# Conditioning panels of a two-block transformer kernel: partial products moved from TensorE to VectorE

## The reference

```python
s_c, s_cc = silu(c), silu(c_ctx)
for i in range(2):
    m  = (s_c  @ ada_w[i] + ada_b[i]).reshape(1, 9, 1, D)     # ada_w: 2 x 1024 x 9216
    mc = (s_cc @ ada_w[i] + ada_b[i]).reshape(9, D)
    x = half_step_ffn(x, m[:, 0], m[:, 1], m[:, 2], ...)      # ctx too, with mc[0..2], in layer 0
    hx = modulate(x, m[:, 3], m[:, 4])                        # hc: ctx with mc[3], mc[4], in layer 0
    y = neighbourhood_attention(hx, hc, ...) if i == 0 else short_conv_mixer(hx, ...)
    x = post_norm_update(x, y, m[:, 5], ...)
    x = half_step_ffn(x, m[:, 6], m[:, 7], m[:, 8], ...)
```

## Time and profile before

| | |
|---|---|
| three runs | 3009.21, 3017.51, 3021.42 us; median 3017.51 |
| profiled execution | 3014.72 us, of which the span of the trace is 3012.9 |
| busy, share of the span | TensorE 96%, weight load 84%, VectorE 59%, ScalarE 45%, GpSimd 12% |
| transfers | 474.79 MB, mean 158 GB/s |
| mean granted TensorE clock | 0.99 |

### The profile page before, as it was taken

The page is one execution under the profiler, slowest core; times in us unless marked ns, Lnnn a source line. Parts: engine busy times, 40 slices in busy tenths (PEclk is TensorE's granted clock), DMA queues, the critical chain, the costliest instruction groups (busy, mean ns, idle before and its releaser), DMA issues. The chain is left out here.

```text
span 3012.9 us, 51229 instructions
## 1 busy us (share of the span) xinstructions
PE 2898.0 (96%) x19396; PEld 2540.7 (84%) x19396; DVE 1765.8 (59%) x2644; ACT 1356.7 (45%) x1928; POOL 375.3 (12%) x306
## 2 busy tenths in 40 slices
PE   6999999899999999999899999999999999999998
PEld 3667765677888889888899989899999998988998
DVE  2323224267766667666545866757855577566784
ACT  1222213125655544554344544455644454436563
POOL 2111100113110110211100120201101002020110
PEclk8999999999999999999999999999999999999999
DMA  9986354751565655465435505245555451533564
GB/s 325 285 252 195 103 164 130 198 168 49 158 184 154 194 183 160 148 195 182 142 120 167 161 28 176 92 134 153 170 162 161 137 154 57 160 114 112 161 179 135
DMA packets 586157, 474.79 MB, mean 158 GB/s; under 512 B 28721, under 2 KB 547889, under 8 KB 585665
## 3 DMA queue, kind: packets, MB, share of 16 engines
q1 hardware_dynamic: 584464, 460.44, 49.8%
q0 software_dynamic: 1520, 11.95, 1.3%
HBM read 471.23 MB, written 4.72 MB: 158 GB/s over the span
## 5 line engine op out<-in xcount | busy, mean ns | idle before, releaser
L2309 DVE TENSOR_TENSOR low<-raw,high 128x1024 fp32r<-128x1024 f32 (+1 forms) x744 | 904.6, 1219 | 801.0 <-ACT high L2079 798.6
L2079 ACT CAST high<-raw 128x1024 fp32r<-128x1024 f32 (+1 forms) x744 | 768.1, 1034 | 987.9 <-PE PS L1987 604.7
L1985 PE MATMUL PS<-NHh,high 128*128 128x272 f32 (+1 forms) x2304 | 669.0, 290 | 11.4 <-DVE NHl L1752 6.9
L1987 PE MATMUL PS<-NHh,low 128*128 128x272 f32 (+1 forms) x2304 | 660.8, 287 | 0.0
L1986 PE MATMUL PS<-NHl,high 128*128 128x272 f32 (+1 forms) x2304 | 660.0, 286 | 0.0
L1985 PEld LDWEIGHTS PS<-NHh,high 128*128 128x128 f32 x2304 | 433.3, 188 | 16.9 <-issue 9.1
L1986 PEld LDWEIGHTS PS<-NHl,high 128*128 128x128 f32 x2304 | 433.9, 188 | 0.8
L1987 PEld LDWEIGHTS PS<-NHh,low 128*128 128x128 f32 x2304 | 433.6, 188 | 0.0
L1983 PE MATMUL PS<-XX,high 128*128 128x512 f32 x966 | 347.8, 399 | 0.0
L1985 PE MATMUL PS<-XX,high 128*128 128x512 f32 (+1 forms) x752 | 273.5, 364 | 6.9 <-DVE XX L2370 4.4
L1982 PE MATMUL PS<-XX,low 128*128 128x256 f32 x966 | 272.4, 282 | 1.4 <-DVE XX L2370 1.0
(11 more groups left out here) (351 smaller groups left out, 4868.7 us busy)
## 6 DMA issues: line engine op xcount, KB each, us to landing
raw<-w_in_dram SPq DMA_DIRECT2D x416, 256.0 KB, 3.0
raw<-ffn_w_in_dram SPq DMA_DIRECT2D x352, 256.0 KB, 3.4
part<-ada_w_dram SPq DMA_DIRECT2D x184, 256.0 KB, 4.2
raw<-w_ffn_in_dram SPq DMA_DIRECT2D x176, 256.0 KB, 3.2
raw<-ffn_w_out_dram SPq DMA_DIRECT2D x160, 256.0 KB, 3.1
raw<-w_branch_dram SPq DMA_DIRECT2D x96, 256.0 KB, 3.0
raw<-w_ffn_out_dram SPq DMA_DIRECT2D x80, 256.0 KB, 3.0
part_sg<-ada_w_dram SPq DMA_DIRECT2D x48, 256.0 KB, 3.0
```

What stands on the lines that cost most here:

```text
L1985: nc.tensor.matmul(out, wh, xh, start=begin, stop=False)
L1987: last = nc.tensor.matmul(out, wl, xh, start=False, stop=end)
L2079: nc.scalar.copy(high[:, slot, 0:nk, :], raw[:, slot, 0:nk, :]).then_inc(s_high, 1)
L2309: nc.vector.tensor_tensor(low[:, slot, 0:nk, :], raw[:, slot, 0:nk, :], high[:, slot, 0:nk, :].bitcast(F32), ALU.subtract).then_inc(s_low, 1)
```

## The change

All panels but the first four are no longer multiplied on TensorE. VectorE multiplies each 128x512 row tile of a part by the matching column of silu(c) (a value for each partition) and adds it to an accumulator of 128x512 in SBUF, one for each panel of the turn; panels 4 to 9 (`ADA_BOTH`) have a second accumulator with silu(c_ctx). This is done in `split_low`, behind the low copy of chunk `HOST[A]` + 4. Once for each turn TensorE sums the accumulators over the partitions against a mask with a single column of ones (`ada_sum`), two chunks behind the host of the turn's last part, at the latest behind chunk 83. SyncE's wait for a part buffer is now for VectorE's accumulation (`s_adak`). The parts are spread anew: 16 over chunks 2 to 13, 16 over 14 to 23, 16 over 24 to 33, 8 over 34 to 39, 72 over 45 to 82. They use 14 buffers: four (later two) during glu, seven from chunk 45, three from 68. The rule of `issue` for a buffer that was used before is the same.

```diff
-ADA_HOSTS = ((0, 32, 80), (44, 24, 24), (68, 16, 24))
+ADA_HOSTS = ((2, 12, 16), (14, 10, 16), (24, 10, 16), (34, 6, 8), (45, 38, 72))
+ADA_BOTH = 10
...
-    return HOST[4 * TURN * t - 1]
+    return min(HOST[4 * TURN * t - 1] + 2, 83)
...
+        ROWS, TAIL, TOP = range(4, 11), 11, (12, 13)
+        part_slot = [A % 4 if HOST[A] < 32 else A % 2 if HOST[A] < 44 else
+                     ROWS[A % 7] if HOST[A] < 68 else 11 + A % 3 for A in range(ADA_PARTS)]
+
+        def ada_acc(t, x, c):
+
+            if c:
+                return acc_both[:, x, :]
+            return (acc2, acc3)[x - 2][:] if x > 1 else (RS if t < 5 else SG)[:, x, :]
...
-            due = HOST[before] + 4 if before is not None else {PSG: 47, PRS: 47, TAIL: 71}.get(part_slot[A], 1)
+            due = HOST[before] + 4 if before is not None else 3 + part_slot[A] if HOST[A] < 44 else 48 if HOST[A] < 68 else 71
...
                 if before is not None:
-                    sp.wait_ge(s_ada, 4 * ADA_FIRST + before + 1)
-                elif slot == PSG:
-                    sp.wait_ge(s_hl, FT + 2)
+                    sp.wait_ge(s_adak, before + 1)
+                elif slot in ROWS:
+                    sp.wait_ge(s_chunk, steps[1]["S0"] + 4)
                 elif slot == TAIL:
                     sp.wait_ge(s_chunk, steps[2]["S0"] + 4)
-                elif slot < 3:
+                elif slot in TOP:
+                    sp.wait_ge(s_res, KT + 4)
+                elif slot == 0:
                     sp.wait_ge(s_ada, 4 * ADA_FIRST)
...
+            def ada_sum(t):
+
+                pe.wait_ge(s_adak, 4 * TURN * t)
+                pe.wait_ge(s_adarow, max(1, t - 1))
+                for c in range(2):
+                    for x in range(TURN):
+                        both = TURN * t + x < ADA_BOTH
+                        if both or not c:
+                            last = nc.tensor.matmul(PS[32 * x:32 * x + 32, ROW_BANK + t % 2, :],
+                                                    ONEW[:, 2 * (TURN - x) - 1 - c:2 * (TURN - x) + 31 - c], ada_acc(t, x, c),
+                                                    start=not c, stop=bool(c) or not both)
+                last.then_inc(s_adasum, 1)
...
-                        for A in ada_parts(S + c):
-                            ada_part(ADA_FIRST + A // 4, A % 4)
+                        if isinstance(S, int) and S + c in sum_after:
+                            ada_sum(sum_after[S + c])
...
                 nc.vector.tensor_tensor(low[:, slot, 0:nk, :], raw[:, slot, 0:nk, :],
                                         high[:, slot, 0:nk, :].bitcast(F32), ALU.subtract).then_inc(s_low, 1)
+                for A in ada_parts(S - NSLOT if isinstance(S, int) else S):
+                    ada_accumulate(A)
+
+            def ada_accumulate(A):
+
+                n, c = ADA_FIRST + A // 4, A % 4
+                t, x = divmod(n, TURN)
+                slot = part_slot[A]
+                dve.wait_ge(s_part[slot], 32 * part_slot[:A + 1].count(slot))
+                if x == 0 and c == 0 and t > 1:
+                    dve.wait_ge(s_adasum, t - 1)
+                for y in range(2):
+                    k = 2 * c + y
+                    src = flat(parts_at[slot][:, 2 * y:2 * y + 2, :])
+                    for e in range(2 if n < ADA_BOTH else 1):
+                        acc, factor = ada_acc(t, x, e), silu[:, KT * e + k:KT * e + k + 1]
+                        if k == 0:
+                            ins = nc.vector.tensor_scalar(acc, src, factor, None, ALU.mult)
+                        else:
+                            ins = nc.vector.scalar_tensor_tensor(acc, src, factor, acc, ALU.mult, ALU.add)
+                        if y == 0 or e < (n < ADA_BOTH):
+                            link(ins)
+                ins.then_inc(s_adak, 1)
+                dve.wait_ge(s_adak, A + 1)
...
-                for c in range(2 if m < 2 else 1):
+                for c in range(2 if m < 1 else 1):
```

More of the change, by code:

```diff
@@ L317, in two_block_kernel @@
         SC0 = 2 * (TURN - 1)
-        SCW = E1.take("SCW", [P, KT, SC0 + 32])
         adarow = E1.take("adarow", [P, T1])[:]
+        acc2 = E1.take("acc2", [P, PW])
+        scw_at = E1.at
+        acc3 = E1.take("acc3", [P, PW])
+        SCW = Region(scw_at).take("SCW", [P, KT, SC0 + 32])
+        ONEW = E1.take("ONEW", [P, 2 * TURN + 31])
+        silu = E1.take("silu", [P, 2 * KT])
         e1_end = E1.at
@@ L325, in two_block_kernel @@
         scf = A3.take("scf", [P, 4 * 2 * KT])
+        both_at = inner + 4 * T1 * 16
+        acc_both = Region(both_at).take("acc_both", [P, TURN, PW])
         parts_at = [Region(at).take(f"part{q}", [P, 4, UW]) for q, at in enumerate(
[L327 to L332, removed]
+            [inner + 4 * T1 * f for f in (20, FT + 20, FT + 18, FT + 16)]
+            + [common_end + 4 * T1 * f for f in (0, 2, 4, 6, KT + 1, KT + 3, KT + 5)]
+            + [inner + 4 * T1 * (2 * FT - 2), inner, inner + 4 * T1 * 2])]
+        ROWS, TAIL, TOP = range(4, 11), 11, (12, 13)
[5 more added lines that the diff above has]
+            return (acc2, acc3)[x - 2][:] if x > 1 else (RS if t < 5 else SG)[:, x, :]
         A4 = Region(inner)
@@ L399, in two_block_kernel @@
         s_chunk = sem("chunks_multiplied")
-        s_ada = sem("ada_parts_multiplied")
+        s_ada = sem("first_ada_parts_multiplied")
+        s_adak = sem("ada_parts_accumulated")
+        s_adasum = sem("ada_panels_summed")
         s_free = sem("units_evacuated")
@@ L514, in issued_after @@
             return [A for A in range(ADA_PARTS) if issue[A] == S] if isinstance(S, int) else ()
+        sum_after = {turn_host(t): t for t in range(1, ADA // TURN)}
         turn_unit = [None] + [unit_of(turn_host(t)) for t in range(1, ADA // TURN)]
@@ L1831, in ada_part @@
             def ada_part(n, c):
[L1833 to L1845, removed]
+                src = raw0[:, 4 * FIRST_PLACE[n] + c]
+                if c == 0:
+                    pe.wait_ge(s_raw0[n], 128)
+                rows, first, final = ROW_BANK + n % 2, n < 2, n >= 2
                 for y in range(2):
@@ L1849, in ada_part @@
                     last = nc.tensor.matmul(PS[32 * g:32 * g + 32, rows, :],
-                                            SCW[:, k, SC0 - 2 * x:SC0 - 2 * x + 32],
+                                            SCW[:, k, SC0 - 2 * n:SC0 - 2 * n + 32],
                                             src[:, 2 * y:2 * y + 2, :].rearrange("p a n -> p (a n)"),
@@ L2383, in ada_rows @@
             def ada_rows(t):
-                dve.wait_ge(s_ada, 4 * TURN * (t + 1))
                 if t:
+                    dve.wait_ge(s_adasum, t)
                     dve.wait_ge(s_adacols, t)
+                else:
+                    dve.wait_ge(s_ada, 4 * TURN)
                 nc.vector.tensor_copy(adarow, PS[:, ROW_BANK + (t % 2 if t else 1), :]).then_inc(s_adarow, 1)
@@ L2417, in _ @@
                 nc.vector.tensor_tensor(SCW[:, :, SC0 + c], cin[:, c, :], sig[:, c, :], ALU.mult).then_inc(s_sc4, 1)
+            link(nc.vector.tensor_tensor(silu[:], cols[:, COLS["c"]:COLS["c"] + 2 * KT], scf[:, 0:2 * KT], ALU.mult))
+            link(nc.vector.memset(ONEW[:], 0.0))
+            link(nc.vector.memset(ONEW[:, 2 * TURN - 1:2 * TURN], 1.0))
             dve.wait_ge(s_ada, 2 * TURN)
```

## The result

| | before | after |
|---|---|---|
| median | 3018.39 us (4 runs, 3009.21 to 3021.42) | 3342.45 us (4 runs, 3340.35 to 3347.16) |
| ratio, 95% interval | | 1.1083 (1.1059 to 1.1107): slower |
| span of the profiled execution | 3012.9 | 3340.8 |
| first res matmul | 342.54 | 512.34 |
| first v matmul | 511.88 | 778.47 |

324 us more, and all of it lies ahead of the scores: they start 329 us later, and what is behind them takes 2343.7 us instead of 2344.8.

What follows compares the result with a forecast made beforehand. TensorE was taken to bound the kernel before; after the change, raw loads waiting in series behind VectorE's accumulations would starve it. Profiled 3014.7 us plus 266.6 gave 3281.3, and 2.8 for the median gave 3284 us, range 3200 to 3350.

Steps and rivals of the forecast that it cites:

- the loop: Raw weight loads queue behind SyncE's wait for VectorE's accumulation, so loading runs one chunk deep despite four raw buffers.
- What bounds it, and what it takes off TensorE: TensorE, busy 96% of the span, is what the end waits for; the change saves it 89 us.
- The order of waits: At nearly every step 6 to 41 and 49 to 84, the next raw load waits for the current chunk's copies and accumulations.
- The multiply-add of 0.75 us: VectorE's 128x512 multiply-add, estimated from other widths at 0.75 us, bounds 0.70 and 0.80.
- The turn: One raw load to the next: 8.13 us plus accumulations, against 5.45 us a chunk on TensorE; 67 waiting turns.
- The milestones: Running sum of delays by stage: res +132 us, v +220, q +266.6.
- The sums cost nothing, the last one its stall: TensorE's earlier accumulator sums cost nothing within the loop's slack; without the loop the last would stall some 5 us.
- the loads that run ahead: Rival: raw loads still run ahead and the 89 us come home, 2928 us; chance 0.08.
- VectorE as the bound: Rival: VectorE alone bounds, 9 us over with both conditioning rows, swallowed by three chunks of lead; about 2935 us; chance 0.02.
- The cheaper loop: Rival: the loop closes but raw loads land 1.0 us sooner in 67 turns, 3217 us; chance 0.13.
- The estimate of 3197: Total if 256 KB raw loads took the Trainium skill's 2.6 us rather than 3.9, making the sum 87 us lower.
- Half clock: Rival: TensorE at 1.2 GHz paces the short turns, 10.3 us a chunk, 18 us more, 3302 us; chance 0.13.

Runs made afterwards that it cites:

- the loop opened: Changed kernel with parts in reused buffers issued up to two steps later (host of the buffer's previous part + 6, capped at own host + 4): 2959.36 us, ratio 0.9809.
- the run with GpSimd later: Changed kernel with one wait added, so GpSimd takes its difference in the first glu stage only after VectorE's accumulations: 3330.07 us, ratio 1.104.
- the run with later sums: Changed kernel with the first three sums on TensorE two chunks later: 3346.58 us, ratio 1.1098.
- the narrow run: Changed kernel with every multiply-add but the first of a panel on 64 of 512 columns: 3250.35 us, ratio 1.0787.

## Why the prediction was right, and where it was off

I forecast 3284 (3200 to 3350), slower; 3342 was measured. The direction and the mechanism hold, and the time is inside the range, but near its end: 324 us against 266.6. The direction and the loop were worked out and are borne out; the range held for loads that took 0.38 us longer, but also for a hold by GpSimd that it was not made for, and that is luck.

- *What bounds it, and what it takes off TensorE*: with the loop opened, the scores start at 610.3 instead of 668.1 us. That is 58 of the 89 us that TensorE alone would save. 12 of the other 31 are the stretch in which VectorE is 95% busy; the rest is open.
- *The order of waits*: right, and shown from both sides. Moving the wait takes away all of the loss (3342 to 2959); a like wait added alone to the kernel before makes 182 us, there with TensorE standing for the parts.
- *The multiply-add of 0.75 us*: the trace reads 750 ns; 784 to 790 ns from start to start in a chain, as each waits for the one before it. I had taken the link as free.
- *The turn:* over 66 of the 67 waiting turns of after, from the end of the parts to the raw issue 0.89 us (said 0.95), high to low copy 1.09 but for a single 5.1 (said 1.08), raw issue to high copy 5.28 (said 4.9, so +25 us). The parts took some 25 us more than their sum by 0.54 and 0.75: 18 of it GpSimd's hold, as the run with GpSimd later takes them away, which no step of mine had, the rest the links. The 66 turns are 777 us where the same sum gives 726: 51 of the missing us. 5 more went ahead of step 7.
- *The milestones:* res 170 us later (I said 132), v 267 (220), q 328 (267). The miss is 38, 47 and 61 us after 34, 54 and 67 waiting turns, fastest in glu, where GpSimd's hold lies. The term that was mis-sized is the turn: 8.13 us plus parts was too short by some 0.77.
- *The sums cost nothing, the last one its stall:* the first half is shown by the run with later sums; the second wasn't tried.
- *What would show it:* SyncE's wait names VectorE, but it is 5.6 us a wait (638 us in 113) and not 7, as a step with two parts has two waits. TensorE waited more for glu's epilogue (93.6 us) than for the low copy (43.5), because the epilogue stands behind the parts on VectorE, and frees the banks. I had named the low copy alone; both hang on the same loop. In glu the low copies are 9.5 to 15.5 us apart (said 9.6 to 14). TensorE's waits in the first 960 us of after:

```profile
PE PS L2009 <- DVE SG L2634: 93.6, 9, 13.4
...
PE PS L2009 <- DVE low L2333: 43.5, 11, 6.1
```

- *The rivals:* the loads that run ahead are what one edited line makes of it. I priced that at 2928 and it came to 2959. VectorE as the bound, 2935 by my account, plays no part in after (47% busy from 70 to 508 us). With the loop open it does: my count had its 9 us of excess swallowed by the lead, and VectorE is 95% busy from 70 to 190 us and costs TensorE 12. The cheaper loop is refuted: from raw issue to high copy it took 5.28 us and not less, though the transfer engines were busy 38%. The estimate of 3197 falls with it; the fit that it uses is stated in the Trainium skill ("DMA: Bandwidth & Descriptors", section Anatomy of one DMA) for transfers that GpSimd issues, and these are SyncE's. Half clock: the granted clock was 0.77 from 70 to 508 us, but TensorE paced next to nothing. If it did, the high copies would wait for it. What they waited for in the first 960 us of after:

```profile
ACT high L2103 <- DMA raw<-ffn_w_in_dram: 386.4, 38, 16.6
ACT high L2103 <- DMA raw<-ffn_w_out_dram: 193.6, 19, 11.7
ACT high L2103 <- DMA raw<-na_w_qkv_dram: 161.5, 19, 12.1
...
ACT high L2103 <- PE PS L2011: 6.1, 3, 2.7
```

The load came last 76 times, TensorE 3 times, for 6 us; VectorE waited 5 us more for the sums.

## What to carry to other kernels

When a wait is moved to another engine, ask what stands behind it in the waiting queue, and how far ahead of its use that is issued. A prefetch is as deep as the oldest thing the issuing queue waits for, not as the number of buffers: here four buffers worked as one, and an issue one step later was worth 348 us and two 383. An engine's busy share over the whole run does not show it. By stage it did: nothing was busy for more than 65%, neither an engine nor the transfers. Then read one turn in order of time. And when such a wait is gone, look by stage for the next limit: here VectorE, 83% busy in the mean and 95% where it mattered.

## What the runs showed of the hardware

- A multiply-add of VectorE (128x512, two inputs in SBUF) that starts while GpSimd runs its operation on SBUF takes 1.75 to 1.78 us instead of 0.75 (12 times), and ends 0.55 us behind GpSimd's. The multiply with one tensor input is held as well, 1.51 us beside 0.49 in the narrow run. It works the other way round too: the low copy, with two inputs, had started first (131.62 against GpSimd's 132.19) and kept its 1.23 us, and GpSimd's operation took 1.81 us, where it takes 1.29 with VectorE idle. The profile books the hold as duration of the held instruction, not as idle time. The Trainium skill has the rule in "SBUF — State Buffer", section Who interferes with whom: VectorE and GpSimd share a port pair that one instruction holds alone, and who comes second is blocked. The trace agrees in both directions, with 1.78 us for 0.75 and 1.81 for 1.29.
- An added wait of SyncE on a semaphore that VectorE counts up anyway, with no work behind it, made the kernel before 6% slower (3198 us instead of 3016).
